# Block-2 attention with two heads a step in an fp32 two-block kernel

## The reference

```python
h = rmsnorm(x, g_mix); proj = h @ w_in          # qa ka va qb kb vb fl qc kc vc qi ki wi gl
# a: stick-breaking, strictly causal
log_1m = where(strict, log_sigmoid(-z), 0); later = cumsum(log_1m, reverse) - log_1m
w = where(strict, exp(log_sigmoid(z) + later), 0);            out_a = w @ va
# b: forgetting, c = cumsum(log_sigmoid(fl + b_forget))
z = q k^T / 8 + c_t - c_s;   p = softmax(where(causal, z, -inf));   out_b = p @ vb
# c: sparse, the 64 best keys of an index score (4 index heads, relu, weighted)
z = q k^T / 8 on the selected keys;   p = softmax(z);         out_c = p @ vc
y = sum_n sigmoid(gl_n) * (out_n @ w_branch[n]);   x = x + y @ w_out
x = x + square(relu(rmsnorm(x, g_mlp) @ w_up)) @ w_down
```

## Time and profile before

| what | us |
|---|---|
| median of 3 runs | 2005.49 (2003.61 to 2008.32) |
| profiled execution, first to last instruction | 2001.7 |
| TensorE busy in it | 1926.1 |
| GpSimd busy | 1373.1 |
| ScalarE busy | 1112.4 |
| VectorE busy | 611.6 |

### The profile page before, as it was taken

How to read it: one execution, slowest core, us unless ns; L and a number is a source line. 1 busy time by engine, 2 the same in 40 slices (tenths; PEclk the granted TensorE clock), 3 DMA queues, 4 the chain that set the end, 5 groups by cost and what they waited for, 6 DMA issues and landing times.

```text
span 2001.7 us, 26129 instructions
## 1 busy us (share of the span) xinstructions
PE 1926.1 (96%) x9524; PEld 1557.7 (78%) x9524; DVE 611.6 (31%) x1121; ACT 1112.4 (56%) x1643; POOL 1373.1 (69%) x573
## 2 busy tenths in 40 slices
PE   6999999999999999999999899999999999999998
PEld 3667787787788777778878677888888777788887
DVE  3212433513245551334334321421114332132112
ACT  3544675334676654467555865554445585555444
POOL 3656788756678777667788444678879744478886
PEclk8999999999999999999989999999999999999999
DMA  9854555744455555445546333455555533345553
GB/s 366 281 199 153 163 167 180 242 127 137 138 163 199 168 157 159 137 144 160 180 136 196 95 95 106 137 172 187 187 168 164 178 97 93 106 147 187 183 187 126
DMA packets 171269, 328.73 MB, mean 164 GB/s; under 512 B 12448, under 2 KB 13600, under 8 KB 171040
## 3 DMA queue, kind: packets, MB, share of 16 engines
q1 hardware_dynamic: 168272, 320.49, 50.4%
q10 hardware_dynamic: 2896, 6.84, 0.9%
HBM read 326.24 MB, written 1.05 MB: 164 GB/s over the span
## 4 chain that ended last, share of the span: by engine, by line
PE 53%; POOL 21%; issue 20%; ACT 3%; DMA 1%; DVE 1%; POOLq 1%; SPq 0%; DVEq 0%; ACTq 0%
POOL wlo L472 21%; PE G L1502 14%; PE G L1504 13%; PE G L1503 13%; PE A L1504 1%; PE A L1503 1%; PE A L1502 1%; PE A L1623 1%; DMA raw<-in_w_in 1%; PE A L1556 1%; DMA modz<-in_w_mod 1%; PE A L1817 1%; PE G L1838 1%; ACT whi L486 1%; PE A L1787 0%
## 5 line engine op out<-in xcount | busy, mean ns | idle before, releaser
L472 POOL TENSOR_TENSOR wlo<-raw,whi 128x1024 fp32r<-128x1024 f32 x568 | 1369.3, 2418 | 614.8 <-ACT whi L486 610.9
L486 ACT ACTIVATE whi<-raw 128x1024 fp32r<-128x1024 f32 x568 | 599.3, 1058 | 655.5 <-PE G L1504 548.1
L1502 PE MATMUL G<-whi,hhi 128*128 128x512 f32 (+1 forms) x1648 | 664.7, 403 | 22.8 <-DVE hlo L1010 11.8
L1504 PE MATMUL G<-whi,hlo 128*128 128x512 f32 (+1 forms) x1648 | 645.6, 392 | 0.0
L1503 PE MATMUL G<-wlo,hhi 128*128 128x512 f32 (+1 forms) x1648 | 645.1, 391 | 0.0
L1502 PEld LDWEIGHTS G<-whi,hhi 128*128 128x128 f32 x1648 | 313.8, 190 | 106.7 <-issue 40.8
L1504 PEld LDWEIGHTS G<-whi,hlo 128*128 128x128 f32 x1648 | 313.8, 190 | 66.8
L1503 PEld LDWEIGHTS G<-wlo,hhi 128*128 128x128 f32 x1648 | 314.6, 191 | 59.3
L1502 PE MATMUL G<-whi,ohi 128*128 128x512 f32 x240 | 94.1, 392 | 1.0 <-issue 1.0
L1503 PE MATMUL G<-wlo,ohi 128*128 128x512 f32 x240 | 93.4, 389 | 0.0
L1504 PE MATMUL G<-whi,olo 128*128 128x512 f32 x240 | 93.4, 389 | 0.0
(11 more groups left out here) (388 smaller groups left out, 2337.8 us busy)
## 6 DMA issues: line engine op xcount, KB each, us to landing
raw<-in_w_in SPq DMA_DIRECT2D x332, 512.0 KB, 3.5
raw<-in_w_up SPq DMA_DIRECT2D x64, 512.0 KB, 3.6
raw<-in_w_down SPq DMA_DIRECT2D x64, 512.0 KB, 3.6
raw<-in_w_out SPq DMA_DIRECT2D x40, 512.0 KB, 4.3
raw<-in_w_branch_out SPq DMA_DIRECT2D x36, 512.0 KB, 4.4
modw<-in_w_mod SPq DMA_DIRECT2D x32, 512.0 KB, 5.1
raw<-in_w_branch SPq DMA_DIRECT2D x24, 512.0 KB, 3.6
modz<-in_w_mod SPq DMA_DIRECT2D x16, 512.0 KB, 10.8
```

The lines of the kernel that those rows point to most:

```text
L472: pool.tensor_tensor(wlo[:, s], raw[:, s], whi[:, s].bitcast(F32), ALU.subtract).then_inc(lo_ready, 1)
L486: act.activation(whi[:, slot], raw[:, slot], ACT.Copy).then_inc(hi_ready, 1)
L1502: pe.matmul(bank, hi, whi[:, slot, kk, 0:n], start=first, stop=False)
L1504: return pe.matmul(bank, lo, whi[:, slot, kk, 0:n], start=False, stop=last)
```

## The change

The loop steps over twelve pairs of heads instead of 24 heads.

- Scores: both heads of a pair are queued alternately, one on the lower and one on the upper half of the array's rows, into the two banks of a pair. Two pairs of banks (`PAIR`) and two sets of SBUF tiles remain.
- Values: v is now the stationary operand (64 columns, so half the array's columns for each head) and the weights move. The outputs arrive turned, in the layout that the branch products want; ScalarE and VectorE split them from PSUM straight into `ohi` and `olo`, one bank (two pairs of heads) at a time. `read_heads` and the turn after the loop are gone.
- Softmax: exponentials stay in PSUM; VectorE multiplies them by the reciprocal of their sums on the way to SBUF, ahead of the transposes.
- Decays: the sums are made three times, on partitions 0, 32 and 64 on; VectorE splits them into three bf16 parts, and one bf16 matmul with a selecting matrix adds the three.
- ScalarE preloads the table set `natural_log_exp_and_others` ahead of the stretch.
- TensorE's order in step i: values of pair i - 2, scores of pair i, sums or transposes of pair i - 1, two slabs. ScalarE serves pair i - 1 first, then pair i, then the splits. At the end the first branch product stands ahead of the last pair's values, and the sigmoids are split in two groups around the first two branch products.

```diff
+PART = 32
+PAIRS = H2 // 2
...
-    head = np.zeros((P, NF, P), np.float32)
+    head = np.zeros((P, NF, P), np.uint16)
     for h in range(NF):
-        head[h, h] = 1
+        head[h:3 * PART:PART, h] = 0x3F80
+    head = head.view(np.float32)
...
-        tmp = sb_at("tmp", [P, 4, 2, 3 * P], F32, eb)
+        tmp = sb_at("tmp", [P, 2, 2, 2, 3 * P], F32, eb)
...
-        HEADS = [A[0], A[1], G[2], G[3]]
+        PAIR = [a_banks[:, 0:2], g_banks[:, 2:4]]
+        OUT = [A[2], A[3]]
...
-        STEPS = 3 * H2
-        LATE_FIRST = 7 * SLOTS - STEPS
+        STEPS = 3 * PAIRS
+        LATE_FIRST = 7 * SLOTS - 2 * STEPS
...
+                act.preload_act_table_set("natural_log_exp_and_others")
...
+                    if 1 <= i <= STEPS:
+                        j = i - 1
+                        bank, own = PAIR[j % 2], tmp[:, j % 2]
+                        if j < PAIRS:
+                            act.wait_ge(sb_cum, w(sb_cum))
+                            act.activation(own[:, 1], bank[:, :, 0:3 * P], ACT.Exp).then_inc(sb_weights, 1)
+                        else:
+                            act.wait_ge(sm_turned, w(sm_turned))
+                            act.activation(own[:, 1], bank[:, :, 0:3 * P], ACT.Copy).then_inc(sm_copied, 1)
                     if i < STEPS:
...
+                        bank, own = PAIR[i % 2], tmp[:, i % 2]
+                        if i < PAIRS:
                             act.wait_ge(sb_scores, w(sb_scores))
...
+                            link(act.activation(own[:, 0], bank[:, :, 0:3 * P], ACT.Abs))
                             link(act.activation(own[:, 0], own[:, 0], ACT.Exp, scale=-1.0))
                             act.activation(own[:, 1], own[:, 0], ACT.Ln, bias=one[:]).then_inc(sb_log, 1)
                         else:
                             act.wait_ge(sm_max, w(sm_max))
...
+                            for b in range(2):
+                                for t, cols in enumerate((slice(0, P), slice(P, 3 * P))):
+                                    ins = act.activation(bank[:, b, cols], bank[:, b, cols], ACT.Exp,
+                                                         bias=nmx[:, 2 * (i % 2) + t, b:b + 1],
+                                                         accum_out=hsum[:, i % 2, t, b:b + 1])
+                            ins.then_inc(sm_exp, 1)
+                    if i >= 2 and i % 2 == 1:
+                        grp, q = divmod((i - 2) // 2, 2)
+                        act.wait_ge(heads_out, w(heads_out))
+                        act.activation(two_kt(ohi[:, grp], 4)[q], OUT[q][:], ACT.Copy).then_inc(split_hi, 1)
+                    if i < STEPS:
+                        for s in range(2):
+                            late_slab(LATE_FIRST + 2 * i + s, late_dst, G[0:2], scale)
+                    if i == STEPS:
+                        act.wait_ge(late_evacuated, w(late_evacuated, 7 * TT))
+                        for c in (0, 2):
+                            sigmoid(c)
+                        branch(0)
+                branch(1)
+                for c in (4, 1, 3, 5):
+                    sigmoid(c)
...
+                dve.memset(fgw[:], 0.0).then_inc(dve_step, 1)
+                dve.wait_ge(dve_step, w(dve_step))
                 dve.wait_ge(forget_log, w(forget_log))
...
+                for n in range(3):
+                    ins = dve.tensor_tensor(fgw[:, :, n, 0:NF], fg[:, 2], fg[:, 1], ALU.subtract)
+                ins.then_inc(forget_ready, 1)
...
+                dve.wait_ge(cum_out, w(cum_out))
+                cum = OUT[1]
+                link(dve.tensor_copy(negc[:], cum[:, 0:S]))
+                link(dve.tensor_tensor(negr[:], cum[:, 0:S], negc[:], ALU.subtract))
+                dve.tensor_copy(negc[PART:2 * PART], negr[PART:2 * PART])
+                link(dve.tensor_copy(negm[2 * PART:], negr[2 * PART:]))
+                dve.tensor_tensor(negc[2 * PART:], negr[2 * PART:], negm[2 * PART:], ALU.subtract).then_inc(cum_copied, 1)
+                for i in range(STEPS + 2):
+                    bank, own = PAIR[i % 2], tmp[:, i % 2]
+                    if i < PAIRS:
                         dve.wait_ge(sb_log, w(sb_log))
...
+                        dve.scalar_tensor_tensor(own[:, 0], bank[:, :, 0:3 * P], 0.0, own[:, 1], ALU.max, ALU.add)\
                            .then_inc(sb_soft, 1)
                         topk_round()
...
+                        topk_round()
+                        if i == PAIRS - 1:
                             dve.tensor_scalar(selb[:], work[:], TAKEN, NEG, ALU.not_equal, ALU.mult).then_inc(selected, 1)
...
+                    elif i < STEPS:
                         dve.wait_ge(sm_scores, w(sm_scores))
...
+                        for t, cols in enumerate(tiles):
+                            ins = dve.reduce_max(nmx[:, 2 * (i % 2) + t], bank[:, :, cols], AX.X, negate=True)
+                        ins.then_inc(sm_max, 1)
+                        dve.wait_ge(sm_exp, w(sm_exp))
+                        link(dve.reciprocal(hrec[:, i % 2], hsum[:, i % 2]))
+                        for t, cols in enumerate(tiles):
+                            n = cols.stop - cols.start
+                            ins = dve.tensor_tensor(own[:, 0, :, cols], bank[:, :, cols],
+                                                    hrec[:, i % 2, t].unsqueeze(2).to_broadcast([P, 2, n]), ALU.mult)
+                        ins.then_inc(sm_normed, 1)
+                    if i >= 2 and i % 2 == 1:
+                        grp, q = divmod((i - 2) // 2, 2)
+                        split_low(two_kt(ohi[:, grp], 4)[q:q + 1], two_kt(olo[:, grp], 4)[q:q + 1], OUT[q:q + 1])
+                merge(lambda c, t: gate2[c][:, t], lambda t, h: y2[:, t, h * CH:(h + 1) * CH], split=False)
...
+                part = fgw[:].rearrange("p t n a -> p t (n a)")
+                pe.matmul(OUT[1][:, 0:S], part[:, 0], upto[:, 0:S], start=True, stop=False, skip_group_check=True)
+                pe.matmul(OUT[1][:, P:S], part[:, 1], upto[:, 0:P], start=False, stop=True, skip_group_check=True).then_inc(cum_out, 1)
+                def head_scores(i):
+                    grp, p = divmod(i, PAIRS)
+                    banks = [PAIR[i % 2][:, b] for b in range(2)]
+                    halves = [rows(b) for b in range(2)]
+                    if grp == 0:
+                        q, k = qa[:, p], ka[:, p]
+                        for bank, r in zip(banks, halves):
+                            pe.matmul(bank[:, 0:S], k[r, 0:P], q[r, 0:S], start=True, stop=False, skip_group_check=True)
+                        for bank, r in zip(banks, halves):
+                            pe.matmul(bank[:, S:3 * P], k[r, P:S], q[r, P:S], start=False, stop=False, skip_group_check=True)
+                        for bank in banks:
+                            pe.matmul(bank[:, 0:P], ident16, strict16, start=False, stop=False, skip_group_check=True)
+                            ins = pe.matmul(bank[:, S:3 * P], ident16, strict16, start=False, stop=True, skip_group_check=True)
+                        ins.then_inc(sb_scores, 1)
+                        return
+                    q, k = (qb[:, p], kb[:, p]) if grp == 1 else (qc[:, p], kc[:, p // 2])
+                    for bank, r in zip(banks, halves):
+                        pe.matmul(bank[:, P:3 * P], q[r, P:S], k[r, 0:S], start=True, stop=False, skip_group_check=True)
+                    for bank, r in zip(banks, halves):
+                        pe.matmul(bank[:, 0:P], q[r, 0:P], k[r, 0:P], start=False, stop=False, skip_group_check=True)
+                    for b, bank in enumerate(banks):
+                        if grp == 1:
+                            pe.matmul(bank[:, 0:P], esel[:, 2 * p + b], negc[:, 0:P], start=False, stop=False, skip_group_check=True)
+                            pe.matmul(bank[:, P:3 * P], esel[:, 2 * p + b], negc[:], start=False, stop=False, skip_group_check=True)
+                        else:
+                            pe.matmul(bank[:, 0:3 * P], ident16, selb[:], start=False, stop=False, skip_group_check=True)
+                        pe.matmul(bank[:, 0:P], ident16, causal16, start=False, stop=False, skip_group_check=True)
+                        ins = pe.matmul(bank[:, 2 * P:3 * P], ident16, causal16, start=False, stop=True, skip_group_check=True)
+                    ins.then_inc(sm_scores, 1)
+                def head_values(j):
+                    grp, p = divmod(j, PAIRS)
+                    weights = tmp[:, j % 2, 1]
+                    out = OUT[p // 2][:, (p % 2) * S:(p % 2 + 1) * S]
+                    for s in range(TT):
+                        for b in range(2):
+                            col = (VA + (2 * p + b) * DH, VB + (2 * p + b) * DH, VC + p // 2 * DH)[grp]
+                            v = z2[:, s, col:col + DH]
+                            if s == 0:
```

(40 more changed lines are left out.)

217 lines of the change are left out of this document (58 added, 159 removed).

## The result

The changed kernel takes 1930.86 us (median of four runs, 1926.67 to 1935.72), the kernel before 2004.55 (four runs, 2003.61 to 2008.32). The ratio is 0.9621, with an interval of [0.9599, 0.9642]. The forecast was 1930.5.

A forecast was written before the change was run, and what follows sets the result against it. TensorE's queue was taken as the bound (busy 96%): 36.2 us a layer saved in the stretch plus 1.3 ahead, 75.0 for two layers; span 2001.7 - 75.0 = 1926.7, plus 3.8 gives 1930.5 us, range 1918 to 1955.

The forecast's parts named there:

- the quarters of the earlier trace: Modulation matmuls on column quarters: four fp32 matmuls overlapped in 0.50 us, from which a pair's values were put at 0.75.
- the sign that the prediction named: In each step of the stretch, the four value matmuls of a pair were to lie within 0.75 us.
- the wait ahead: Ahead of the stretch TensorE waited 1.2 us for ScalarE's copy of the decays; moving it was to free 1.3.
- The covers: Time between a pair's chain ending and TensorE needing its result: 3.6 us forecast for softmax, 2.7 for stick-breaking.
- The ring of weights: GpSimd's weight slabs: two a step need 2 x 2.4 us in a step of 8.5, so no bound.
- T: End of a pair's scores; softmax chain to end at T + 4.9, stick-breaking chain at T + 6.4.
- Rival D: Two buffers aren't enough: each step waits 1 to 2 us, with clock dips; 12 to 30 a layer, 1955 to 1990; chance 0.05.
- rival E: Waits in every step keep the clock at 1.2 GHz through both stretches; kernel slower, 2140; chance 0.04.
- Rival B: ScalarE's tables still switch, making it late every second stick-breaking step; 2 to 5 a layer, 1934 to 1941; chance 0.05.
- with two the chain ends at T + 9.0: With two table loads a stick-breaking pair, the chain ends just in time, TensorE being back at T + 9.1.
- Rival C: VectorE meets GpSimd in three subtractions and five splitting instructions; seven at 2.45 us cost 10 a layer, 1950; chance 0.06.
- The offset: The median of the runs was taken to lie 3.8 us above the profiled span (2005.5 - 2001.7).

The follow-up runs named there:

- e1: The changed kernel with a pair's scores made one head after the other, each head followed by its own masks; 1951.45 us, ratio 0.9731.
- e3: The changed kernel with the second head's values put behind the score matmuls in ten steps; 1946.44 us, ratio 0.9703.
- e4: The changed kernel with the decays alone put back to one fp32 copy and fp32 matmuls of 8 rows; 1941.34 us, ratio 0.9685.
- e8: The kernel before with only the preload of the table set with exp and log added; 1995.99 us, ratio 0.9942.
- e5: The changed kernel without the preload of the table set; 1931.72 us, ratio 0.9618.
- e6: The changed kernel with VectorE's multiplication by the reciprocal sums made three times; 1929.18 us, ratio 0.9613.
- e7: The changed kernel with VectorE's multiplication by the reciprocal sums made seven times; 1981.43 us, ratio 0.9871.
- e2: The changed kernel with both matmuls of one head queued before the other head's, in scores and values; 1929.96 us, ratio 0.9626.

## Why the prediction was right, step by step

**The bound.** TensorE's queue was the bound and stayed it; the count of its work gave 104.8 for the stretch and 104.55 was measured. 75.0 for two layers stands against 76.4.

**The terms.** With the durations of the trace after: slabs 12 x 5.65 = 67.8 (forecast 68.4), values and scores 12 x 1.65 = 19.8 (19.2), stick-breaking masks 4 x 0.23 = 0.9 (0.8), decays or selection with masks 8 x 0.565 = 4.5 (4.2), sums 4 x 1.71 = 6.8 (6.9), transposes 8 x 0.58 = 4.6 (5.3). The sum is 104.4. Values were put at 0.75, by the quarters of the earlier trace rows; they took 0.80, a little outside the sign that the prediction named. The likely reason is a change of the array's shape for each pair that I had shared out to the scores; no run isolates it. Transposes were put at 0.33 a head, and six take 0.58 and not 0.66; the 0.08 has the size of such a change, now paid once a pair. Errors of 0.1 to 0.7 in both directions cancel, so that the total is nearer than its terms.

**The parts of the gain.** Undone one at a time, the stretch grows by 11.3 (e1), 7.8 (e3) and 5.9 (e4). The preload is worth 6.5 in the kernel before (e8), the wait ahead 1.4, and the drain 5.8: 24 transposes at 3.3 (at the full clock, as in e8) and two waits of 0.8 and 1.7 that the trace of before shows there. The sum is 38.7, against 37.7 measured. It doesn't add up exactly, and two things are known of that. By the durations of before, the scores, the values and the decays were worth 10.2, 7.4 and 5.4, which is 2.0 less than undoing them costs; changes of shape that each edit brings along are a likely reason, not a shown one. Slabs and transposes, which no experiment undoes, became shorter by 0.6 and 0.7. Nor is the 6.5 the preload's own: without it (e5) the changed kernel gains as much.

**The covers.** The ring of weights was no bound, as forecast: TensorE waits for no low part in the stretch or in the 260 us behind it; the wait later in the layer is 1.1, where it was 0.5 before. Softmax, VectorE and then ScalarE in the changed kernel:

```profile
1171.30 1.02 DVE L1454 TENSOR_REDUCE nmx<-G 128x2 f32<-128x256 f32 x2 [3.04 <-PE G L1965]
1174.41 0.18 DVE L1457 RECIPROCAL hrec<-hsum 128x4 f32<-128x4 f32 x1 [2.09 <-ACT G L923]
1174.62 1.02 DVE L1460 TENSOR_TENSOR tmp<-G,hrec 128x256 f32<-128x256 f32 x2
```
```profile
1171.96 0.81 ACT L911 ACTIVATE tmp<-A 128x768 f32<-128x768 f32 x1 [1.92 <-PE A L2015]
...
1174.15 0.22 ACT L923 ACTIVATION_READ_ACCUMULATOR G<-G,nmx 128x1 f32 x1
```

T is 1171.10. The chain ends at 1175.64, T + 4.5 (forecast 4.9), and TensorE asks at 1179.55, T + 8.45 (8.5): cover 3.9 against 3.6, confirmed by e6 and e7. In stick-breaking the second pair's addition ends at 1139.9 and TensorE asks at 1142.71: 2.8 against 2.7. Rival D was no danger, and with no waits in the stretch the granted clock stayed at 1.00, so rival E had nothing to start from.

**Rival B** was priced wrongly, and e5 shows it: 2 to 5 us a layer were forecast for tables that still switch, and it is nothing. The step that failed is "with two the chain ends at T + 9.0": it put both loads into the chain, where the one ahead of the exp runs before T, in time that ScalarE has left. It also put ScalarE's work at 9.1 us in a plain step and up to 10 in one with an evacuation, where the trace has 7.8 and 9.57.

**Rival C** came true in one instruction of the eight that it counted. VectorE's decays in the changed kernel, and GpSimd beside them:

```profile
1126.75 0.28 DVE L1436 CAST negc<-negr 32x256 bf16<-32x256 f32 x1
1127.05 2.41 DVE L1437 CAST negm<-negr 64x256 bf16<-64x256 f32 x1
1129.50 0.42 DVE L1438 TENSOR_TENSOR negc<-negr,negm 64x256 bf16<-64x256 f32 x1
1129.95 0.96 DVE L1445 SCALAR_TENSOR_TENSOR tmp<-A,tmp 128x768 f32<-128x768 f32 x1
```
```profile
1126.83 2.49 POOL L481 TENSOR_TENSOR wlo<-raw,whi 128x1024 fp32r<-128x1024 f32 x1 [0.91 <-ACT whi L495]
1130.91 2.38 POOL L481 TENSOR_TENSOR wlo<-raw,whi 128x1024 fp32r<-128x1024 f32 x1 [1.59 <-ACT whi L495]
```

The conversion that starts 0.22 after GpSimd's instruction lasts until GpSimd is done; the one 0.08 ahead of it takes 0.28, and the one in GpSimd's next gap 0.42. The first pair's addition ends at 1130.9, TensorE asks at 1133.47, and 2.6 us of cover are left. The trace agrees with the Trainium skill (SBUF — State Buffer, "Who interferes with whom"): one of the five was caught, for about 2.4 us, where the prediction had said one or two. The three subtractions fell in a gap of GpSimd, as forecast, and together took 0.34. The clearest pair is one that the diff leaves alone: the two mask additions that took 2.45 each while GpSimd worked from 1110.45 on the earlier trace rows now run almost wholly in a gap of GpSimd (1120.50 to 1120.82), in 0.29 and 0.28:

```profile
1120.39 0.29 DVE L1418 TENSOR_TENSOR work<-work,half 128x128 f32<-128x128 f32 x1
```

**The offset.** The 3.8 between the profiled span and the median was two things: 1.8 or 1.9 lies around every span (2003.61 against 2001.7; 1935.72 against 1933.9 in the changed kernel), the other 1.9 was the place of the profiled execution among its runs. It held, in part by luck, because the spans of the changed kernel (1924.9, 1927.9, 1930.2, 1933.9) scatter about 1929.05, 2.3 above the 1926.7 of the sum. The layers themselves gave 76.4 where the sum had 75.0, while the medians show 73.7; the 2.7 between them have the size of the scatter at the start. So the agreement of 0.4 us in the time is better than the method; the 37.5 a layer against 37.7 and 38.7 is what it can do.

## What to carry to other kernels

Where one engine is busy for nearly the whole span, price its queue from starts of neighbouring groups in the trace, changes of shape included; twelve steps came out 0.25 us from the forecast of 104.8. Then give every other engine's chain its own clock within a step, and put a delay into the chain only from the point at which its engine would otherwise be idle. Matmuls that fill half the rows or half the columns go in pairs, with nothing of full height or width between them; and waits of the matmul engine that come back in every step are priced above their length: here at one and a half times on the whole, with the extra almost all behind the waits above 2 us.

## What the runs showed of the hardware

- Halves of TensorE's array, by rows or by columns, take one head's or two heads' matmuls in the same time: 0.85 us (e1) and 0.80 (e3). The order in the queue changes the stretch by 0.15 us at most (e2), and in the changed kernel two column halves write one bank.
- I had not expected that taking the preload away would leave the length of a layer unchanged to 0.01 us while two table loads of 1.28 us came back in every pair (e5): ScalarE had the time.
- Waits of 16.6 us brought 8.2 us more of TensorE's own time with them (e7). After a wait of 3.40 the matmuls of the next 3 us ran at the low level; the steps behind waits of 0.7 to 1.6 had a granted clock of 1.00.
- A conversion in SBUF on VectorE took 2.41 us when it started 0.22 behind GpSimd's instruction, and a smaller one 0.28 when it started 0.08 ahead of it; the same mask addition took 2.45 before and 0.29 after.
- The start of the kernel scatters by up to 9.0 us between executions (first index head at 1103.22 in e2, at 1112.26 in the changed kernel), with a DMA of the modulation and with the granted clock, while the length of a layer repeats to a few hundredths.
